# Seven block products per pair of weight units in the down half of a feed-forward layer, one PSUM bank at a time

## What is computed

```python
def sq_relu_ffn(x, w1, w2):
    return jnp.square(jax.nn.relu(x @ w1)) @ w2          # w1: 1024x4096, w2: 4096x1024

x = layer_norm(DN_ALPHA * x + mix, ln1_g[i], ln1_b[i])
x = layer_norm(DN_ALPHA * x + sq_relu_ffn(x, ffn_w1[i], ffn_w2[i]), ln2_g[i], ln2_b[i])
```

## Time and profile before

| | |
|---|---|
| median of 3 runs | 1677.28 us (1677.14 to 1677.29) |
| profiled execution, span from first to last instruction | 1675.7 us; what lies around the span is not in the trace |
| PE busy | 1657.4 us, 99% of the span, 12242 matmuls |
| DVE, ACT, POOL busy | 915.7, 526.4, 697.9 us |
| granted TensorE clock, mean | 0.997 |

### The profile page before, as it was taken

One profiled execution on the slowest core, in us unless ns is written; L12 is line 12 of the kernel. 1 busy time (PEld: TensorE's weight loads), 2 busy tenths in 40 slices (PEclk: granted clock), 3 DMA queues, 4 the chain that ended last, 5 costly groups with the idle time before them and its releaser, 6 DMA issues.

```text
span 1675.7 us, 31321 instructions
## 1 busy us (share of the span) xinstructions
PE 1657.4 (99%) x12242; PEld 1619.5 (97%) x12242; DVE 915.7 (55%) x1720; ACT 526.4 (31%) x883; POOL 697.9 (42%) x577
## 2 busy tenths in 40 slices
PE   9999999999999999999999999999999999999996
PEld 9999999999999999999999788999999999999996
DVE  7789999999756441322226624895365531313225
ACT  4555545565224330311202512221024411303105
POOL 0000000000456565555555365455556565565552
PEclk9999999999999999999999999999999999999998
DMA  5223333323222222222222322322222222222222
GB/s 195 82 96 102 101 102 101 97 75 107 73 89 77 82 82 88 75 88 88 77 88 88 115 87 87 96 70 76 82 83 76 88 79 85 87 77 88 84 80 70
DMA packets 44453, 149.16 MB, mean 89 GB/s; under 512 B 5056, under 2 KB 10816, under 8 KB 43072
## 3 DMA queue, kind: packets, MB, share of 16 engines
q1 hardware_dynamic: 37888, 129.98, 23.3%
q10 hardware_dynamic: 6464, 17.74, 3.4%
HBM read 142.55 MB, written 5.15 MB: 88 GB/s over the span
## 4 chain that ended last, share of the span: by engine, by line
PE 98%; DVE 1%; ACT 1%; DMA 0%; issue 0%; ACTq 0%; DVEq 0%
PE ps L656 80%; PE ps L922 5%; PE ps L642 2%; PE ps L643 2%; PE ps L644 2%; PE ps L825 1%; PE ps L808 1%; PE ps L994 1%; PE ps L802 1%; PE ps L800 1%; PE ps L815 1%; DMA xr<-x 0%; PE ps L944 0%; PE ps L945 0%; PE ps L855 0%; PE ps L676 0%
## 5 line engine op out<-in xcount | busy, mean ns | idle before, releaser
L656 PE MATMUL ps<-h,wh 128*128 128x288 f32 x2944 | 506.5, 294 | 0.0
L560 POOL TENSOR_TENSOR wl<-wraw,wh 128x1024 fp32r<-128x1024 f32 x184 | 450.2, 2447 | 15.3
L656 PEld LDWEIGHTS ps<-h,wh 128*128 128x128 f32 x2944 | 427.9, 188 | 0.7 <-issue 0.7
L557 POOL TENSOR_TENSOR tick<-tick 128x1 f32<-128x1 f32 x184 | 44.8, 243 | 900.0 <-DMA wraw<-wstream 466.7
L656 PE MATMUL ps<-xh,wh 128*128 128x288 f32 x1888 | 409.1, 298 | 0.0
L656 PE MATMUL ps<-xl,wh 128*128 128x288 f32 x1888 | 406.8, 297 | 0.0
L656 PE MATMUL ps<-xh,wl 128*128 128x288 f32 x1888 | 406.2, 297 | 0.0
L656 PE MATMUL ps<-h,wl 128*128 128x288 f32 x1472 | 311.9, 293 | 0.0
L656 PEld LDWEIGHTS ps<-xh,wl 128*128 128x128 f32 x1888 | 306.0, 189 | 0.0
L656 PEld LDWEIGHTS ps<-xh,wh 128*128 128x128 f32 x1888 | 304.7, 189 | 1.3 <-issue 1.2
L656 PEld LDWEIGHTS ps<-xl,wh 128*128 128x128 f32 x1888 | 304.8, 189 | 0.0
(11 more groups left out here) (257 smaller groups left out, 1892.5 us busy)
## 6 DMA issues: line engine op xcount, KB each, us to landing
wraw<-wstream SPq DMA_DIRECT2D x240, 512.0 KB, 3.4
acb<-acum_scratch ACTq DMA_DIRECT2D x8, 1152.0 KB, 6.1
out_y<-r SPq DMA_DIRECT2D x8, 288.0 KB, 2.3
xr<-x ACTq DMA_DIRECT2D x4, 288.0 KB, 6.4
xr<-x SPq DMA_DIRECT2D x4, 288.0 KB, 6.3
hs<-ssm_in ACTq DMA_DIRECT2D x8, 128.0 KB, 6.0
out_ssm_s<-hsn ACTq DMA_DIRECT2D x8, 128.0 KB, 6.1
out_ssm_p<-hp ACTq DMA_DIRECT2D x8, 128.0 KB, 1.9
```

Of the source, the lines that this page charges most:

```text
L557: pool.tensor_tensor(m.tick[:, 1:2], m.tick[:, 0:1], m.tick[:, 0:1], ALU.add)
L560: pool.tensor_tensor(m.wl[:, s], m.wraw[:, s], m.wh[:, s], ALU.subtract).then_inc(S.w_ready, 1)
L656: last = mm(m.ps[:, 2 * s + h, 0:moving.shape[-1]], part, moving, start=(k, n) == (0, 0), stop=(k, n) == (KT - 1, 2))
```

## The change

For chunks 0, 1 and 2 of each layer, two down units (output tiles 2p and 2p+1) form a *pair*. The pair's product is read as a 2x2 block product: weights in two halves of the 1024 inputs by two output tiles, hidden values in two halves of the inputs by two token halves. It is computed with seven block products in place of eight (the Winograd form), each of 4 tiles x 3 parts = 12 matmuls, one product after the other, each wholly into one bank. The product of the first blocks is accumulated over chunks 0 to 2 in its own bank (4 + p) and folded in at chunk 2. Chunk 3 keeps eight products. The seven products need sums of hidden values (4 blocks per up pair) and of weights (3 half units per pair), and the high and low parts of these.

The order of the steps changes to interleave: up (1,0) runs before down 0, then up (1,1) to (1,3) and up (2,0), then down 1, and so on; down 3 follows up (3,3). Loops are written out. In down pairs of chunks 0 to 2, ACT rounds the weights and POOL only does the seven low parts of half a unit each; without `tick`: in this order, each 128x512, the low part of `wl` a (low half), of sum 1, of `wl` b (low half), of sum 2, of `wl` a (high half), of sum 4, of `wl` b (high half).

```diff
-FFN_BLOCKS = [("up", 0), ("up", 1), ("down", 0), ("up", 2), ("down", 1), ("up", 3), ("down", 2), ("down", 3)]
+FFN_STEPS = [("up", 0, 0), ("up", 0, 1), ("up", 0, 2), ("up", 0, 3), ("up", 1, 0), ("down", 0, None),
+             ("up", 1, 1), ("up", 1, 2), ("up", 1, 3), ("up", 2, 0), ("down", 1, None),
+             ("up", 2, 1), ("up", 2, 2), ("up", 2, 3), ("up", 3, 0), ("down", 2, None),
+             ("up", 3, 1), ("up", 3, 2), ("up", 3, 3), ("down", 3, None)]
+RESIDUALS = {(0, 0): (0,), (0, 1): (1, 2), (0, 2): (3, 4), (0, 3): (5, 6), (1, 0): (7,)}
...
+    def split_sums(q, u):
+        pool.wait_ge(S.w_hi, u + 1)
+        pool.wait_ge(S.ws_sum, 4 * q + 3)
+        low(m.wl[:, a, 0:HALF], m.wraw[:, a, 0:HALF], m.wh[:, a, 0:HALF]).then_inc(S.ws_lo, 1)
+        n = weight_sum(q, 0)
+        pool.wait_ge(S.ws_hi, 4 * q + 1)
+        low(m.sum_l[n][:, :], m.sum_s[n][:, :], m.sum_h[n][:, :]).then_inc(S.ws_lo, 1)
...
+    def sum_products(layer, c, p, u0):
...
+        pe.wait_ge(m.slot_evac[s0], slot_turn(u))
+        pe.wait_ge(S.ws_lo, 5 * q + 2)
+        terms((bank_p, wh_a, wl_a, 0, 0, c == 0, c == 2),
+              (bank_b, m.sum_h[n1], m.sum_l[n1], 0, 3, True, True)).then_inc(S.st_done, 1)
+        pe.wait_ge(m.slot_evac[s1], slot_turn(u + 1))
+        pe.wait_ge(S.ws_lo, 5 * q + 4)
+        terms((bank_c, wh_b, wl_b, 0, 4, True, True),
+              (bank_d, m.sum_h[n2], m.sum_l[n2], 0, 5, True, True)).then_inc(S.st_done, 1)
+        pe.wait_ge(S.st_acc, 3 * q + 1)
+        pe.wait_ge(S.ws_lo, 5 * q + 5)
+        pe.wait_ge(S.w_ready, u + 1)
+        terms((bank_a, wh_a, wl_a, 4, 1, True, True),
+              (bank_b, m.sum_h[n4], m.sum_l[n4], 0, 2, True, True)).then_inc(S.gemm_done, 1)
+        pe.wait_ge(S.st_acc, 3 * q + 2)
+        pe.wait_ge(S.w_ready, u + 2)
+        terms((bank_c, wh_b, wl_b, 4, 6, True, True)).then_inc(S.gemm_done, 1)
...
+    def weight_sums_hi(q, u):
+        f(m.wh[:, a], m.wraw[:, a], ACT.Copy).then_inc(S.w_hi, 1)
+        act.wait_ge(S.ws_sum, 4 * q + 1)
+        f(m.sum_h[n1][:, :], m.sum_s[n1][:, :], ACT.Copy).then_inc(S.ws_hi, 1)
+        act.wait_ge(S.ws_sum, 4 * q + 3)
+        f(m.wh[:, b, 0:HALF], m.wraw[:, b, 0:HALF], ACT.Copy).then_inc(S.ws_hi, 1)
+        f(m.sum_h[n2][:, :], m.sum_s[n2][:, :], ACT.Copy).then_inc(S.ws_hi, 1)
+        act.wait_ge(S.ws_sum, 4 * q + 4)
+        f(m.sum_h[n4][:, :], m.sum_s[n4][:, :], ACT.Copy).then_inc(S.ws_hi, 1)
+        f(m.wh[:, b, HALF:UNIT], m.wraw[:, b, HALF:UNIT], ACT.Copy).then_inc(S.w_hi, 1)
...
+    def hidden_sums(layer, c, i):
+        tt(to[:, 3:5], m.hq[:, :, 1], m.hq[:, 0], ALU.subtract).then_inc(S.hid_sum, 1)
+        dve.wait_ge(S.hid_sum, 3 * n + 1)
+        tt(to[:, 5], m.hq[:, 1, 1], to[:, 3], ALU.subtract).then_inc(S.hid_sum, 1)
+        dve.wait_ge(S.hid_sum, 3 * n + 2)
+        tt(to[:, 6], m.hq[:, 1, 0], to[:, 5], ALU.subtract).then_inc(S.hid_sum, 1)
+        dve.wait_ge(S.hid_hi, 2 * hidden_pair(layer, c, i) + 2)
+        hidden_low(lo[:, 0], m.hq[:, 0, 0], hi[:, 0])
+        hidden_low(lo[:, 1:3], m.hq[:, 1], hi[:, 1:3]).then_inc(S.hid_lo, 1)
...
+    def hidden_sums_lo(layer, c, i):
+
+        dve.wait_ge(S.hid_sum_hi, pair_of(layer, c, i) + 1)
+        hidden_low(hidden_place(m, c, i, 1)[:, 3:7], m.hid_s[(4 * c + i) % HSLOTS][:, 3:7],
+                   hidden_place(m, c, i, 0)[:, 3:7]).then_inc(S.hid_sum_lo, 1)
...
+    def weight_sums(q, u, which):
+        if which == 0:
+            dve.wait_ge(m.w_in[b], 16 * ((u + 1) // RING + 1))
+            tt(s1, a21, a22, ALU.add).then_inc(S.ws_sum, 1)
+            dve.wait_ge(S.ws_sum, 4 * q + 1)
+            tt(s2, s1, a11, ALU.subtract).then_inc(S.ws_sum, 1)
+            tt(a21, a11, a21, ALU.subtract).then_inc(S.ws_sum, 1)
+        else:
+            wait(dve, S.st_done, 2 * q)
+            tt(s4, a12, s2, ALU.subtract).then_inc(S.ws_sum, 1)
+    def down_pair(layer, c, p, u0):
+        dve.wait_ge(S.st_done, 2 * q + 1)
+        tt(second, repeat(bank_b, 2), second, ALU.add).then_inc(S.st_acc, 1)
+        if p < 3:
+            weight_sums(q + 1, u + 2, 0)
+        dve.wait_ge(S.st_done, 2 * q + 2)
+        tt(upper, repeat(bank_c, 2), upper, ALU.add).then_inc(S.st_acc, 1)
+        if p < 3:
+            weight_sums(q + 1, u + 2, 1)
+        if c == 0:
+            cp(d, bank_d).then_inc(S.st_acc, 1)
+        else:
+            tt(d, bank_d, d, ALU.add).then_inc(S.st_acc, 1)
+        if c == 2:
...
+            tt(r11, bank_p, r11, ALU.add).then_inc(S.st_fold, 1)
+            dve.wait_ge(S.st_acc, 3 * q + 3)
+            tt(d, bank_p, d, ALU.add).then_inc(S.st_fold, 1)
+            dve.wait_ge(S.st_fold, folds + 2)
+            tt(r12, r12, d, ALU.add).then_inc(S.st_fold, 1)
+            tt(upper, upper, repeat(d, 2), ALU.add).then_inc(S.st_fold, 1)
+        dve.wait_ge(S.gemm_done, u + 1)
+        tt(lower, bank_pair(m, s0), lower, ALU.add).then_inc(m.slot_evac[s0], 1)
+        dve.wait_ge(S.gemm_done, u + 2)
+        tt(half_of(m.r, 2 * p + 1, 0), bank_c, half_of(m.r, 2 * p + 1, 0), ALU.add).then_inc(m.slot_evac[s1], 1)
...
+            if kind == "up":
+                normalized(layer, c, i, 0, u0)
+                if i == 0 and c > 0:
+                    for which in range(2):
+                        weight_sums(pair_of(layer, c - 1, 0), u0 + DOWN_AT[c - 1], which)
+                for k in RESIDUALS.get((c, i), ())[0:1]:
+                    residual_tile(layer, k)
+                normalized(layer, c, i, 1, u0)
+                if c == 3 and i > 0:
+                    hidden_tiles_lo(layer, i)
+                elif c < 3 and not (i == 0 and c > 0):
+                    hidden_sums(layer, c, i)
+                for k in RESIDUALS.get((c, i), ())[1:2]:
+                    residual_tile(layer, k)
+                if c < 3 and not (i == 0 and c > 0):
+                    hidden_sums_lo(layer, c, i)
```

More of the change, by code:

```diff
@@ L365, in __init__ @@
+        self.mr = put("mr", [P, 2, HT], offset=t0 + 14 * row)
+        self.mean = put("mean", [P, 2, HT], offset=t0 + 15 * row)
+        self.na = put("na", [P, 4, HT], offset=t0 + 23 * row)
+        self.te = put("te", [P, 2, T], offset=t0 + 23 * row)
+        self.dsum = put("dsum", [P, 4, HT], offset=t0 + 23 * row)
         self.again = put("again", [P, 2, 2 * KT], offset=t0 + 25 * row)
         self.cd = put("cd", [P, 2, 2], offset=t0 + 25 * row + 128)
+        part = 7 * HT * 4
+        places = [(h0 + 2 * part * n, h0 + 2 * part * n + part) for n in range(4)]
@@ L682, in last_block @@
+    def last_block(n, u0, xh, xl, half=half_of, first=0):
+        run_few(u0 + first, 6 - first, xh, xl, half=half)
         for h in range(2):
@@ L1339, in end_norm, with hidden_unit @@
             affine(1, pair)
+    def hidden_unit(layer, c, i, j, u0):
+        u = u0 + UP_AT[c, i] + j
+        e, n = 2 * hidden_pair(layer, c, i) + j, hidden_pair(layer, c, i)
+        act.wait_ge(S.gemm_done, u + 1)
+        f(m.cd[:, j], m.ps[:, 2 * (u % 2) + 1, HT:HT + 2], ACT.Copy).then_inc(S.cd_ready, 1)
+        act.wait_ge(S.t_ready, e + 1)
+        f(m.ta[:, j], m.ta[:, j], ACT.Relu, bias=m.cd[:, j, 1:2], scale=-1.0).then_inc(S.rl_ready, 1)
+        act.wait_ge(S.rl_ready, e + 1)
+        wait(act, S.hid_lo, n)
+        f(m.hq[:, j], halves(m.ta[:, j]), ACT.Square).then_inc(S.hid_ready, 1)
+        hi = hidden_place(m, c, i, 0)
+        if c < 3:
+            out, src = (hi[:, 0], m.ta[:, 0, 0:HT]) if j == 0 else (hi[:, 1:3], halves(m.ta[:, 1]))
+        else:
+            out, src = hi[:, 2 * j:2 * j + 2], halves(m.ta[:, j])
+        f(out, src, ACT.Square).then_inc(S.hid_hi, 1)
@@ L1341, in ffn @@
     def ffn(layer, u0):
[L1342 removed]
+        for kind, c, i in FFN_STEPS:
             if kind == "up":
[L1344 to L1362 removed]
@@ new lines, in ffn @@
+                hidden_unit(layer, c, i, 0, u0)
+                if i == 0 and c > 0:
+                    weight_sums_hi(pair_of(layer, c - 1, 0), u0 + DOWN_AT[c - 1])
+                hidden_unit(layer, c, i, 1, u0)
+                if c < 3 and not (i == 0 and c > 0):
+                    hidden_sums_hi(layer, c, i)
+                for k in RESIDUALS.get((c, i), ()):
+                    normed_residual(layer, k)
+            elif c < 3:
+                for p in range(1, 4):
+                    weight_sums_hi(pair_of(layer, c, p), u0 + DOWN_AT[c] + 2 * p)
+                    if p == 1 and c < 2:
+                        hidden_sums_hi(layer, c + 1, 0)
@@ L2047, in ffn @@
             else:
-                block(u0 + 8 * b, "add", 2 * layer + 1)
+                down_block(layer, c, u0 + DOWN_AT[c])
     residual_first(U_WOUT + 6, 0, 0, 6)
```

404 lines of the change are left out of this document (259 added, 145 removed).

## The result

The kernel after takes 1732.2 us (median of four runs, 1731.8 to 1734.9) against 1677.3 us: 1.0331 times the time of before, 95% interval 1.0316 to 1.0346. It is slower, as forecast, and 7.7 us above the forecast of 1724.5.

The account below looks back on a forecast made before the run. TensorE, busy 99%, bounds the kernel before; after the change the port shared by DVE and POOL makes it wait. Stalls 79.0 less 31.8 for removed matmuls give +47.2 on 1677.3: 1724.5 us, 8-in-10 range 1650 to 1748.

Parts of the forecast that it names:

- Matmuls: Down pairs of chunks 0 to 2: 84 matmuls instead of 96, at 0.1325 us each; six blocks give -31.8 us.
- The shared port: Down pairs: DVE's SBUF sums and POOL take turns, holding it 11.15 of 11.13 us before hidden sums, so TensorE waits.
- the walk: Step-by-step timing of each chunk's up pairs and down block: 39.5 us of stall per layer, 79.0 in two.
- up 0: Chunk 0's up pairs, with two residual tiles each in pairs 1 to 3: stalls of 1.05, 6.5 and 1.1 us.
- start of blocks 0, 1, 2: Before each down block's first product, TensorE waits for sums, roundings and POOL's first two low parts: 6.6, 4.8, 4.8 us.
- inside block 0: Within chunk 0's down block, after its start: 4.6 us of stall.
- inside block 1: Chunk 1's down pairs: 0.6 us late, 1.95 at `second`, then 0.65, 0.6 and 0.7; together 4.5.
- inside block 2: Chunk 2's down pairs: folds add four DVE operations before `lower`; next pair start 3.1 us late, then 1.2 each.
- All hidden: Rival: DVE's and POOL's turns fall well and only block starts stall, 6 x 1.3; -24 us, 1653; chance 0.27.
- Port as a sum alone: Rival: POOL falls behind within its reserve, DVE is never late by itself; six blocks +4 us, 1681; chance 0.15.
- Lateness: Rival: lateness carries over, so up pairs of chunks 1 and 2 stall as well; 1748 us; chance 0.12.
- The single bank: Rival: matmuls run into one bank are slower, 0.1335 us and more; 2016 cost 2 us over the sum; no own chance.

Follow-up runs that it names:

- the second experiment: Kernel after, with POOL's seven half-unit operations reading one operand, without the subtraction (output wrong): 1694.9 us, ratio 1.0101.
- the fold experiment: Kernel after, with chunk 2's four folds moved behind `lower`, the add that frees bank pair s0: 1718.2 us, ratio 1.0241.
- the combination: Kernel after, with hidden sums' low part owed past the next unit's first steps, folds behind `lower`, three weight-sum low parts on DVE: 1705.7 us, ratio 1.0170.
- the fourth experiment: Kernel after, with weight sums and roundings for the coming down block ahead of the first unit's normalising in up (c+1,0): 1730.5 us, ratio 1.0313.

## Why the prediction was right, and where its sizes were off

*Matmuls.* The pace in a product without a wait is 0.1327 (taken: 0.1325), so 2016 x 0.1327 = 267.5 us against 24 x 12.45 = 298.8: -31.3, where I had -31.8.

*The shared port* is what makes DVE late inside the down blocks, shown twice: by the turns in the trace and by the second experiment. At the block starts, DVE's, ACT's and POOL's lists in a row and the port both play a part, as the walk had it, and their shares were not separated. POOL's half takes 1.29 when alone (taken: 1.25), and DVE's sums stretch to 1.4 to 1.8.

*The stalls*, layer 0 of the kernel after, predicted and measured:

| | predicted | measured |
|---|---|---|
| up 0 | 1.05 + 6.5 + 1.1 | 1.05 + 5.8 |
| start of blocks 0, 1, 2 | 6.6, 4.8, 4.8 | 5.1, 3.7, 4.0 |
| inside block 0 | 4.6 | 1.7 |
| inside block 1 | 4.5 | 2.6 |
| inside block 2 | 3.1 + 1.2 + 1.2 | 2.5 + 2.7 + 2.5 + 0.8 |
| sum | 39.5 | 32 |

Layer 1 sums to 34: 66 us in all, where I had 79. The walk put nearly every stall in its place (the third one in up 0 did not come) and, but for block 2 and the first of up 0, each of them too high, those inside block 0 by the most. In blocks 0 and 1 I let the lateness of one pair pass on to the next; the trace shows DVE idle for 1.2 and 3.1 us before later `second`s (621.67, 633.61), so it catches up there. In block 2 the folds cost as much in the second and third pair as in the first, since they meet POOL's turns in each: the fold experiment gave back 14 us, where my 3.1 + 1.2 + 1.2 makes 11 in two layers.

*The clock* is the term that was missing. Eight waits of 3.6 to 6 us (up 0 and three block starts a layer), and one of 3.3 inside layer 1's block 2, are each followed by 10 to 23 matmuls at 0.24, and in seven of the nine the first interval is 0.38. Counted by spacing this is 18 us, and the slower first intervals behind the other waits make it 19. The sum -31.3 + 66 + 19 = 54 stands beside a span longer by 55.0. The counted 19 are not all to be had: of those in down blocks, the experiments bear out 1.7 to 2.0 each where DVE and POOL have room, and in the kernel after filling the waits gave nothing. So two errors of size, 13 too much and 19 too little, nearly cancelled; that 1724.5 came so close is partly luck. It also hid one of the signs named: TensorE's busy share fell to 96%, not to some 94, because slow matmuls count as busy.

*The rivals.* All hidden (1653) fell. Port as a sum alone (1681) fell too, but not everywhere. Two windows of the kernel after, from the first product of a down block to the next up unit, chunks 0 and 2:

```profile
591.81:641.36 49.55, 48.53 (x337) 47.68 (x338) 32.10 (x39) 15.74 (x23) 42.33 (x32) 0.94 0.22 65
801.01:856.50 55.49, 47.76 (x336) 46.85 (x337) 40.84 (x52) 13.93 (x21) 44.04 (x32) 0.95 0.20 63
```

The blocks of chunks 0 and 1 last 49.1 to 49.5 us from there, close to that rival's 50.3 less the 1.3 of the start, with POOL busy for 42 of them. What it lacked is ahead of these windows, 5.1, 3.7 and 4.0 us of waiting at the starts and 6.8 in up 0, and in chunk 2, where the block takes 55.5 us (56.8 in layer 1) and not 51. Lateness did not carry into the up pairs of chunks 1 and 2 (1748): there is no gap there. The single bank costs 0.3 us by its pace, less than the 2 allowed for.

*Open.* How the up pairs of chunk 0 could be freed of their 4 us, the combination's largest remaining item beside block 0's start, was not tried: the two residual tiles per pair would have to go to a place where DVE has room.

## What to carry to other kernels

A product that saves one matmul in eight adds sums on the engines that feed TensorE; before making it, count not only their busy time but each turn at what they share, along the chain from one bank's release to the next. In a list worked through in order, put the operation that frees a bank or feeds the next product ahead of everything that nobody waits for: here that alone gave 14 us. But follow every edge of such a move: the weight sums first, on top of the combination, cost 16 us, and 8 of them came back when the low part that is needed sooner stood ahead of the three low sums. And price a wait of several microseconds on TensorE at more than its length, since here what followed ran at the lower clock, 1.7 to 2.0 us a time where feeding had room.

## What the runs showed that I had not expected

In the kernel after, the matmuls behind the folds' waits of 2.5 us are 0.13 apart from the second on (816.97, 817.20, 817.33); behind those of 3.6 us and more they aren't. The length of a wait does not settle it alone. In the thirteen traces of this kernel and its edits each of the 69 waits of 3.4 us and more is followed by a stretch at the lower clock, but so are 10 of the 35 of 2.2 to 2.7 us, as in chunk 2 of the fourth experiment, behind 2.3 us at 830.49. The same idle time cut into small pieces was cheaper here: gaps of 22.5 us cost 1705.7, gaps of 23.5 us 1713.5.

A POOL operation with one operand of 512 columns takes 0.70 us on average against 1.29 with two undisturbed. It still takes turns with DVE's sums. In the second experiment, POOL's operation that meets DVE's L2282 (623.01 to 623.74) takes 1.04, where the one behind it, undisturbed, takes 0.61:

```profile
623.18 1.04 POOL L644 TENSOR_SCALAR sum_l<-sum_s 128x512 fp32r<-128x512 f32 x1
624.19 0.61 POOL L644 TENSOR_SCALAR wl<-wraw 128x512 fp32r<-128x512 f32 x1
```

The turns are shorter, not absent: the fold L2314 averages 1.06 us there, 1.55 in the kernel after, and 0.76 is a 576-column sum left alone.
